# Six modulation pairs moved inside the mixer, norm's sums in two parts, first slab tile by tile

## The reference, cut to what matters

```
mod = silu(c) @ w_ada + b_ada            # 9 vectors of 1024: shift, scale, gate, three times
u = modulate(rmsnorm(h)); h += 0.5*g1*swiglu(u)        # ffn1, hidden 2816
u = modulate(rmsnorm(h)); h += g2*mixer(u)             # projections, gated delta rule, w_out
u = modulate(rmsnorm(h)); h += 0.5*g3*swiglu(u)        # ffn2
```

## Time and profile before

| | us |
|---|---|
| median of 3 runs | 1472.65 |
| lowest, highest | 1468.71, 1475.05 |
| the profiled execution, its own time | 1471.88 |
| its span | 1470.1 |
| TensorE busy in it | 1389.4 |
| VectorE, ScalarE, GpSimd busy | 856.0, 714.7, 701.4 |

### The profile page before, as it was taken

How to read it: one execution, slowest core, us unless ns; L and a number is a source line. 1 busy time by engine, 2 the same in 40 slices (tenths; PEclk the granted TensorE clock), 3 DMA queues, 4 the chain that set the end, 5 groups by cost and what they waited for, 6 DMA issues and landing times.

```text
span 1470.1 us, 28415 instructions
## 1 busy us (share of the span) xinstructions
PE 1389.4 (95%) x11871; PEld 1247.1 (85%) x11871; DVE 856.0 (58%) x1300; ACT 714.7 (49%) x1149; POOL 701.4 (48%) x805
## 2 busy tenths in 40 slices
PE   6999999898998998999999989789999999999998
PEld 2787887788987887978888879788899999888998
DVE  3544444686977347664554586767643585676533
ACT  2654532674444333445555546555544466555442
POOL 0555453432333223455565453436665543566653
PEclk9999999999999999999999999999999999999999
DMA  9777677453334352457555634335555544455651
GB/s 339 264 251 264 236 272 276 83 179 104 117 101 159 120 170 79 152 182 248 196 170 186 235 122 139 115 120 187 181 196 188 174 133 143 146 185 187 201 187 44
DMA packets 234445, 258.19 MB, mean 176 GB/s; under 512 B 8457, under 2 KB 211663, under 8 KB 234319
## 3 DMA queue, kind: packets, MB, share of 16 engines
q1 hardware_dynamic: 230272, 252.35, 52.1%
q10 hardware_dynamic: 4047, 4.04, 1.4%
HBM read 253.75 MB, written 2.62 MB: 174 GB/s over the span
## 4 chain that ended last, share of the span: by engine, by line
PE 80%; DVE 11%; ACT 4%; DMA 2%; issue 2%; POOL 0%; DVEq 0%; SPq 0%; ACTq 0%
PE ps L680 33%; PE ps L674 24%; PE ps L676 12%; PE ps L921 2%; PE ps L644 2%; DVE w_lo L1869 2%; DMA raw<-in_w_in 2%; ACT w_hi L1280 1%; PE ps L714 1%; PE ps L965 1%; PE ps L653 1%; DMA raw<-in_w_ada 1%; DVE mt L2091 1%; DVE sil L2091 1%; DVE u_hl L1926 1%
## 5 line engine op out<-in xcount | busy, mean ns | idle before, releaser
L626 POOL TENSOR_TENSOR w_lo<-raw,w_hi 128x256 fp32r<-128x256 f32 x800 | 700.9, 907 | 751.5 <-ACT w_hi L1280 751.5
L1280 ACT CAST w_hi<-raw 128x1024 fp32r<-128x1024 f32 (+1 forms) x408 | 411.4, 1044 | 178.1 <-PE ps L680 114.5
L674 PE MATMUL ps<-u_hl,w_hi 128*128 128x512 f32 x1216 | 428.7, 396 | 6.3 <-issue 4.6
L680 PE MATMUL ps<-u_hl,w_hi 128*128 128x256 f32 x1856 | 353.2, 291 | 12.5 <-POOL w_lo L626 4.4
L1869 DVE TENSOR_TENSOR w_lo<-raw,w_hi 128x1024 fp32r<-128x1024 f32 x204 | 268.1, 1315 | 141.0 <-ACT w_hi L1280 140.1
L676 PE MATMUL ps<-u_hl,w_lo 128*128 128x256 f32 x1216 | 340.5, 280 | 0.0
L680 PEld LDWEIGHTS ps<-u_hl,w_hi 128*128 128x128 f32 x1856 | 293.2, 195 | 28.0 <-issue 10.9
L674 PEld LDWEIGHTS ps<-u_hl,w_hi 128*128 128x128 f32 x1216 | 227.9, 187 | 67.0 <-issue 12.9
L680 PE MATMUL ps<-u_hl,w_lo 128*128 128x256 f32 x928 | 264.6, 285 | 1.3 <-issue 1.3
L676 PEld LDWEIGHTS ps<-u_hl,w_lo 128*128 128x128 f32 x1216 | 229.6, 189 | 0.3 <-issue 0.2
L680 PE MATMUL ps<-mid_hl,w_hi 128*128 128x256 f32 x1024 | 182.6, 282 | 0.0
(11 more groups left out here) (368 smaller groups left out, 1527.2 us busy)
## 6 DMA issues: line engine op xcount, KB each, us to landing
raw<-in_mlp_w SPq DMA_DIRECT2D x64, 1024.0 KB, 5.1
raw<-in_w_ffn_up SPq DMA_DIRECT2D x44, 1024.0 KB, 5.1
raw<-in_w_ada SPq DMA_DIRECT2D x36, 1024.0 KB, 7.0
raw<-in_w_in SPq DMA_DIRECT2D x30, 1024.0 KB, 5.2
raw<-in_w_ffn_down SPq DMA_DIRECT2D x16, 1024.0 KB, 5.4
raw<-in_attn_w_in SPq DMA_DIRECT2D x12, 1024.0 KB, 5.0
raw<-in_mlstm_w_in SPq DMA_DIRECT2D x12, 1024.0 KB, 5.0
raw<-in_w_ffn_down SPq DMA_DIRECT2D x8, 768.0 KB, 4.6
```

The source lines that it names most:

```text
L626: pool.tensor_tensor(w_lo[half][:, kt, :], src[:, kt, :], w_hi[half][:, kt, :].bitcast(F32), ALU.subtract).then_inc(low_ready(n, h)[0], 1)
L674: pe.matmul(two(b - 10 + m), x, z, start=(first and kt == ks.start), stop=False, skip_group_check=True)
L680: mm = pe.matmul(bank(b)[:, m * S:(m + 1) * S], a, z[c] if type(z) is tuple else z[:, c, :], start=(first and m == 0 and kt == ks.start an ...
L1280: act.copy(w_hi[t % HALVES][:, 0:k, :], src).then_inc(hi_ready, 1)
```

## The change

- Pairs 10 and 11 leave the four down groups of ffn1, pair 13 the slab list; 13 runs behind `squares` at the seam ffn1 to mixer, 10 at `a5` and 11 at `s3c` of the first heads (behind the fill there), 14 at a new place `a0` before the second heads, 15 at `s3c` of the second heads, 17 at the seam mixer to ffn2. Their row copies and `mod_sums` stay in list order (`with_ada`), 16 and 17 have theirs in the first steps of ffn2. Pairs 10 and 11 are no longer in `APART`.
- The two seams run two `warm` matmuls each instead of four.
- `squares` can be called for tiles (0, 1) and (6, 7) apart; a pair, or half of one, stands between.
- Where a half slab waits for `u` tile by tile (`ready[2] == 1`), the loop is tile by tile, both column halves within each tile.

```diff
-ADA = {"f1": (.., {0: 9, 1: 10, 2: 11, 3: 12}, {1: 9, 2: 10, 3: 11, 4: 12}), "f2": ({1: 17}, {}, {})}
+ADA = {"f1": (.., {0: 9, 3: 12}, {1: 9, 4: 12}), "f2": ({}, {}, {})}
+PAIRS = (2, 3, 0, 1, 4, 5, 6, 7, 8, 9, 12, 13, 10, 11, 14, 15, 16, 17)
+PAIR_AT = {(0, "a5"): 10, (0, "s3c"): 11, (1, "a0"): 14, (1, "s3c"): 15}
-APART = (4, 5, 6, 7, 8, 9, 10, 11, 12, 16, 17)
+APART = (4, 5, 6, 7, 8, 9, 12, 16, 17)
-FIRST = [("qkv", (0, 0)), ("z", 0), ("qkv", (0, 1)), ...
+FIRST = [("qkv", (0, 0)), ("z", 0), ("mod", 13), ("qkv", (0, 1)), ...
-                + [("ga", j) for j in range(4)] + [("ya", 0), ("ya", 1)], {10: 13, 13: 14, 16: 15})
+                + [("ga", j) for j in range(4)] + [("ya", 0), ("ya", 1)], {0: 10, 10: 11, 11: 14, 21: 15})
...
-            def ada_sums(p):
-                b = open_bank("ada", p)
-                for a in range(2):
+            def ada_sums(p, halves=(0, 1)):
+                b = open_bank("ada", p) if 0 in halves else plan.bank("ada", p)[0]
+                for a in halves:
...
-                for m in range(2):
-                    for kt in ks:
+                by_tile = ready and ready[2] == 1
+                for m, kt in [(m, kt) for kt in ks for m in range(2)] if by_tile else [(m, kt) for m in range(2) for kt in ks]:
...
+                    if g == 3 and then not in LATE:
+                        squares(then, (0, 1))
                     if g in downs:
                         ada_sums(downs[g])
                 if then not in LATE:
-                    squares(then)
+                    squares(then, (6, 7))
...
                 if pair:
-                    ada_sums(pair)
-                if then and then not in LATE:
-                    squares(then)
-                if pair:
-                    mod_sums(pair)
+                    squares(then, (0, 1))
+                    ada_sums(pair, (0,))
+                    squares(then, (6, 7))
+                    ada_sums(pair, (1,))
...
+                        if (hh, place) in PAIR_AT:
+                            ada_sums(PAIR_AT[hh, place])
+                    fill("a0")
                     delta(hh, fill)
...
             ffn("f1", "ffn1", "mix")
-            warm(4)
+            ada_sums(13)
+            warm(2)
             mixer()
-            warm(4)
+            warm(2)
+            ada_sums(17)
             ffn("f2", "ffn2", "attn")
...
+                if name == "ffn2":
+                    row_out(16)
                 shifted(name)
+                if name != "ffn1":
+                    row_out({"mix": 13, "ffn2": 17}[name])
```

More of the change, by code:

```diff
@@ L213, in ffn @@
                 plan.group("mod", ups[i - 1])
+            if name == "f2" and i < 2:
+                plan.group("mod", 16 + i)
         for g in range(4):
@@ L254, in make_plan @@
     plan.ada(16)
-    plan.group("mod", 16)
+    plan.ada(17)
     ffn("f2", A["w_ffn2_up"][0], A["w_ffn2_down"][0])
@@ L281 @@
 PAIRED = ("f1", "f1d", "f2", "f2d", "m0", "m1")
-APART = (4, 5, 6, 7, 8, 9, 10, 11, 12, 16, 17)
+APART = (4, 5, 6, 7, 8, 9, 12, 16, 17)
 def turn(p):
-    return (p + 2) % 4 if p < 4 else p
+    return PAIRS.index(p)
 def with_ada(items, pairs):
@@ L297, in with_ada @@
         out += [("ada", p) for j, p in pairs.items() if i == j]
-    return out
-FIRST = [("qkv", (0, 0)), ("z", 0), ("qkv", (0, 1)), ("z", 1)] + [("qkv", (0, j)) for j in range(2, 6)]
+    return out + [("mod", p) for j, p in pairs.items() if j + 3 >= len(items)]
+FIRST = [("qkv", (0, 0)), ("z", 0), ("mod", 13), ("qkv", (0, 1)), ("z", 1)] + [("qkv", (0, j)) for j in range(2, 6)]
 FILL = with_ada([("c", 0), ("c", 1)] + [("qkv", (1, j)) for j in range(6)]
@@ L377, in build @@
         arow += [at(f"arow{2 + i}", [P, 512], F32, big + 24 * KB + 2112 * i) for i in range(2)]
+        arow += [at(f"arow{4 + i}", [P, 512], F32, big + 82 * KB + 2 * KB * i) for i in range(2)]
         mt2 = at("mt2", [P, 2, S], F32, big + 84 * KB)
@@ L454, in row_at @@
         def row_at(p):
-            return arow[p % 2 + (2 if 13 <= p < 16 else 0)]
+            return arow[p % 2 + (4 if p in (10, 13) else 2 if p in (11, 14, 15) else 0)]
         def cs2(name):
@@ new lines, in half @@
+                by_tile = ready and ready[2] == 1
+                for m, kt in [(m, kt) for kt in ks for m in range(2)] if by_tile else [(m, kt) for m in range(2) for kt in ks]:
+                    if m == 0 and h:
+                        pe.wait_ge(sem, count - (ks.stop - 1 - kt))
+                    if m == 0 and ready and kt % ready[2] == 0:
+                        pe.wait_ge(ready[0], ready[1] + (k0 + kt) // ready[2] + 1)
+                    x, y = (w[i][:, kt - ks.start, m * P:(m + 1) * P] for w in (w_hi, w_lo))
+                    z = hl(k0 + kt)
+                    if b >= 10:
+                        o = bank(b - 10 + m)
+                        pe.matmul(two(b - 10 + m), x, z, start=(first and kt == ks.start), stop=False,
+                                  skip_group_check=True)
+                        mm = pe.matmul(o[:, 0:S], y, z[:, 0, :], start=False, stop=(last and kt == ks.stop - 1),
+                                       skip_group_check=True)
+                        continue
+                    for q, (a, c) in enumerate(((x, 0), (x, 1), (y, 0))):
+                        mm = pe.matmul(bank(b)[:, m * S:(m + 1) * S], a, z[c] if type(z) is tuple else z[:, c, :],
+                                       start=(first and m == 0 and kt == ks.start and q == 0),
+                                       stop=(last and kt == ks.stop - 1 and q == 2), skip_group_check=True)
@@ L699, in warm, with squares @@
                     pe.matmul(bank(7), cs("ident"), cst[:, 0:512], start=True, stop=True, skip_group_check=True)
-            def squares(norm):
+            def squares(norm, tiles=(0, 1, 6, 7)):
                 v = NORMS.index(norm)
-                pe.wait_ge(s("sum_ready"), v + 1)
-                for k in (0, 1) if norm in LATE[:-1] else (0, 1, 6, 7):
+                if 0 in tiles:
+                    pe.wait_ge(s("sum_ready"), v + 1)
+                for k in (0, 1) if norm in LATE[:-1] else tiles:
                     if k == 6:
@@ L730, in ffn @@
                         mod_sums(ups[i - 1])
+                    if name == "f2" and i < 2:
+                        mod_sums(16 + i)
                 for g in range(4):
@@ L2002, in ffn @@
                         mod_out(ups[i - 1])
+                    if name == "f2" and i in (1, 2):
+                        mod_out(15 + i)
                 mid_low(10)
@@ L2146, in fill_pieces @@
                         conv(6 * before[1][0] + before[1][1], 1)
+                if due is not None:
+                    mod_out(due)
             def mixer():
```

15 lines of the change are left out of this document (6 added, 9 removed).

## The result

The changed kernel takes 1484.2 us (median of 20 runs, 1477.4 to 1488.6). The kernel before, run beside it 20 times, takes 1478.5; the ratio is 1.004, 95% interval 1.0023 to 1.0057. So it is some 6 us slower, where 3 us less were forecast (1469.6, range to 1476). Its profiled execution (1471.9) stands near the fast end of these. The error of sign is the change's own.

What follows compares the result with a forecast made beforehand. TensorE, busy 1389.4 of 1470.1 us, was taken as the bound. Terms summed to -6.6, plus 3.5 for clock falls gave -3.1: 1468.8 from the profiled 1471.88, a median of 1469.6 us, range 1458 to 1476.

Steps and rivals of the forecast that it cites:

- Step 2: Seam ffn1 to mixer: pair 13 replaces two warm matmuls, its columns vanish in the 2.02 us decay-row wait; 0 us.
- Step 9: Seam mixer to ffn2, and ffn2: half a pair and pair 17 go, pair 16's columns come, second slab delayed; -1.3 us.
- Step 3: At `a5`: `c1` waits for `c0`'s bank, pair 10 runs there, -0.4 us; pair 10's columns in a dense stretch, +0.9.
- Step 1: ffn1 down: two pairs and two column groups leave a stretch without gaps; -5.5 us.
- Step 4: End of first heads: pair 11 fills 1.57 us, `gb0` waits for `z3`'s bank, held up by `gb1`'s load; +2.7 us.
- Step 5: At `gb1`: it still waits for `gb0`'s eviction, now with pair 14's row copy in front; +0.6 us.
- Step 6: At `gb2`: the 2.74 us wait, the columns in front and the low clock behind go; -5.2 us.
- Step 8: End of second heads: `ya0` waits for `ga3`, its second half for pair 15's row copy; +4.7 us.
- Step 7: Pair 15 and its columns leave a dense stretch; -2.8 us.
- The clock: Five idle stretches new or longer; two falls to low clock taken, +3.5 us, bounds 0 and 9.0.
- That the banks would not bite: Rival, chance 0.24: ScalarE evicts early enough at `c1`, `gb0`, `gb1` and `ya0`; -14.8 us in all, median 1458.
- Low clock behind each new gap: Rival, chance 0.17: low clock after all five new or longer idle stretches, costing 11.5 us; +4.9 in all, 1477.6 us.

## Why the prediction was wrong

- **Step 2 failed, by its second half.** It has pair 13's columns "fall ahead of the 2.02 us wait for the decay rows and vanish in it". They did not come alone: a column group takes a turn of banks 0 and 1, and the slab behind it was thrown onto `z0`'s bank. These two neighbours stood in the list of changed turns ahead of the forecast and were given no price, while the same mechanism was priced at `c1`, `gb0`, `gb1` and `ya0`. The rows for it were in the trace of before: ScalarE began to evict `z0` 5.8 us after TensorE had started the slab that now needs its bank (TensorE, then ScalarE):

```profile
276.50 0.50 PE L680 MATMUL ps<-u_hl,w_hi 128*128 128x256 f32 x2
```

```profile
282.34 0.60 ACT L1386 ACTIVATE zs<-ps 128x512 f32<-128x512 f32 x1
```

  Measured: +7.8 for 0, of which gap and columns are 5.43 + 0.9 - 2.02 = 4.3, 2.0 are the low clock around the gap, and 1.5 the stretch at 0.50 from 270.3 us on, which begins ahead of the columns. Banks 5 and 6 for pair 13 give 5.6 us back.
- **Step 9 failed in ffn2.** It counted pair 17 out and pair 16's columns in, and never asked who empties bank 6 between two column groups. +4.2 for -1.3: the wait of 2.42, 1.7 for the stretch at 0.50 behind it, and 1.6 for the wider spacing from 695 us on, which no other run's trace has: within 0.2 the difference of 5.5. The seam itself came out at -0.4. One step later for the columns gives 5.3 us back.
- **Step 3** was right at `a5` to a tenth (gap of 2.56 forecast as 2.6, net -0.4), and too low for the columns of 10: +2.0 for +0.9. The next slab waits 0.83 for VectorE's `mod_out(10)`, the third case of a bank that a column group holds:

```profile
377.77 0.50 PE L685 MATMUL ps<-u_hl,w_hi 128*128 128x256 f32 x2 [0.83 <-DVE modc L1894]
```

- **Steps 1, 4, 5, 6 and 8** came out within 0.4 us, with the gaps foreseen: 3.05 before `gb0` (forecast as a start at 451.4 in place of 449.0, in sum +2.7 for +2.7), none before `gb2`, 2.67 and 3.94 at `ya0` (2.6 and 4.2). Step 7 was right but for two idle stretches of before that have no releaser.
- **The clock.** The forecast took two falls more, 3.5 us. Over the runs it is 12 us more at 0.50, some 6 us. Most of this goes with the two missed waits (51 us are left in the run without them). With the waits known the sum would have been -6.6 + 4.3 + 2.4 + 1.1 = +1.2 of work; measured are -0.4 +/- 0.6. With the two waits mended the work falls by 8.2 us, and the time by 7: without its two waits the change wins more than was forecast.
- **The rivals.** That the banks would not bite (0.24) fell at every one of its places. Low clock behind each new gap (0.17) was near in size (4.9 us more were forecast for it, 5.7 came). In the changed kernel's trace only one of its five places, the 3.94 us before `ya0`'s second half, was followed by 0.50 directly. With the two waits mended `c1`'s 2.56 was too, and so was the gap before `gb0` (2.96), a sixth new idle stretch that the paragraph on the clock leaves out; the 2.67 at `ya0` and the 2.61 at ffn2's second slab were not:

```profile
332.70:336.00 3.30, 3.30 (x18) 3.30 (x17) 2.82 (x7) 0.72 (x2) 0.00 (x0) 0.50 0.96 302
448.80:452.00 3.20, 3.17 (x15) 3.17 (x16) 0.97 (x2) 3.19 (x3) 0.00 (x0) 0.50 0.16 56
567.00:570.00 3.00, 3.00 (x32) 2.86 (x32) 1.43 (x3) 0.00 (x0) 0.00 (x0) 1.00 0.02 5
652.00:655.00 3.00, 3.00 (x19) 2.62 (x18) 2.35 (x3) 2.19 (x3) 3.00 (x4) 1.00 0.02 5
```

  In other runs those two were as well: the gap of 2.62 at ffn2's second slab in the run with the row of 15 early, the 2.67 at `ya0` in the run with four warm matmuls:

```profile
650.70:653.90 3.20, 3.20 (x12) 2.71 (x11) 2.13 (x3) 1.99 (x3) 3.20 (x4) 0.50 0.01 4
571.80:575.00 3.20, 2.78 (x13) 2.78 (x14) 2.42 (x3) 0.37 (x1) 0.00 (x0) 0.50 0.04 11
```

  So one trace does not settle it. Here is each gap over all the traces that have it, with the number in which 0.50 stood at its end or began within 2.2 us:

| gap | us | followed by 0.50 |
|---|---|---|
| second slab of the mixer | 1.58 | 0 of 8 |
| columns of 17 | 2.42 | 3 of 3 |
| `c1` | 2.6 to 2.9 | 7 of 10 |
| `ya0` | 2.7 | 2 of 11 |
| second slab of ffn2 | 2.5 to 2.6 | 2 of 7 |
| `gb0` | 3.0 to 3.3 | 6 of 7 |
| `ya0`'s second half | 3.9 | 6 of 6 |
| second `qkv` slab | 5.43 | 4 of 4 |

  The rule of the Trainium skill weighed in the prediction (*TensorE: Matmul & The Clock Gate*, how oscillation bites in real kernels) says that long enough waits bring the low clock back each time. The traces agree from 3.9 us on. Between 2.5 and 3.3 us it came in some runs and not in others, at one and the same gap; the place matters more than the length (the three traces without it at `c1` are those that still have the wait of 5.43), and no run here says why. The prediction's two falls were read from one trace, where each of its gaps could show only one of the two outcomes.

## What to carry to other kernels

Where groups share banks in turn, every group that is put in or taken out changes the partner of all that follow: list the new neighbours, and for each one read off the old trace when the eviction of the one ends and when the other starts. A list without a time at each entry has not been used. Column groups are as much part of that list as large ones, and of a moved pair its small last part made both losses here; a pair's own place was a wash (10 and 11 gained nothing that the runs can show by moving), so fix the waits around it before looking for a better place.

## What the runs showed of the hardware

One and the same program ran from 1468.7 to 1485.0 us (35 runs of the kernel before), and its mean clock with it (0.988 in its profiled run, 0.984 in the mean). Time x clock spreads less, with a standard error of 0.4 where that of the time is 0.6 (before) and 0.8 (changed). A difference of half a per cent can be read in it, and a single profile can't be compared with another until the stretches at 0.50 are subtracted: in the first 62 us alone, before most of the change had a part, they were 3.4 to 17.1 us long. The same holds for what follows a gap: behind one of 2.6 us at one place, 7 of 10 traces have 0.50 and 3 have 1.00.
